# Weight work of the seven-product pairs, one step later

## The reference

```python
# block 1
ff = einsum('blf,fd->bld', square(relu(einsum('bld,df->blf', h, w_ff1))), w_ff2)   # f = 4096
# block 2
gt, up = split(h @ w1, 2, axis=-1)
y = (silu(gt) * up) @ w2                                                            # hidden width 2816
```

## Time and profile before

| | |
|---|---|
| median of 3 runs | 3332.22 us (3330.53 to 3332.47) |
| the profiled execution, its own time | 3330.85 us |
| its span | 3329.2 us |
| mean granted TensorE clock | 0.995 |
| PE busy | 3213.3 us, 97% |
| DVE busy | 1928.0 us, 58% |
| ACT busy | 1248.0 us, 37% |
| POOL busy | 910.2 us, 27% |

### The profile page before, as it was taken

The page is one execution under the profiler, slowest core; times in us unless marked ns, Lnnn a source line. Parts: engine busy times, 40 slices in busy tenths (PEclk is TensorE's granted clock), DMA queues, the critical chain, the costliest instruction groups (busy, mean ns, idle before and its releaser), DMA issues.

```text
span 3329.2 us, 40301 instructions
## 1 busy us (share of the span) xinstructions
PE 3213.3 (97%) x15473; PEld 2600.4 (78%) x15473; DVE 1928.0 (58%) x2500; ACT 1248.0 (37%) x1855; POOL 910.2 (27%) x567
## 2 busy tenths in 40 slices
PE   8999999999999999899999999999999999999997
PEld 6788777877886788777768788787788678888775
DVE  6762455444317887766653336572463587777676
ACT  3212444444325444444433333312343443334442
POOL 2111222222342222222422124341255222222214
PEclk9999999999999999999999999999999999999998
DMA  3544344325422545544424223214264223234444
GB/s 134 165 104 146 130 134 142 127 74 205 139 95 101 187 168 202 184 151 152 159 101 148 90 76 133 83 69 157 78 216 166 82 95 126 102 120 169 158 136 146
DMA packets 140906, 445.30 MB, mean 134 GB/s; under 512 B 14944, under 2 KB 24544, under 8 KB 137120
## 3 DMA queue, kind: packets, MB, share of 16 engines
q1 hardware_dynamic: 139680, 439.11, 37.9%
q10 hardware_dynamic: 1040, 3.67, 0.3%
HBM read 303.59 MB, written 142.15 MB: 134 GB/s over the span
## 4 chain that ended last, share of the span: by engine, by line
PE 50%; DVE 12%; issue 2%; ACT 2%; DMA 1%; POOL 0%; SPq 0%; DVEq 0%; ACTq 0%; POOLq 0%
PE pair L2253 24%; PE pair L332 19%; PE pair L451 3%; DVE act_lo L2455 1%; DVE f1hl L2455 1%; DVE f2hl L2455 1%; DMA w_raw<-in_stream 1%; DVE wide L2102 1%; DVE w_lo L2126 1%; PE bank L662 1%; PE wide L842 1%; PE bank L810 0%; PE wide L575 0%; PE wide L1521 0%; DVE act_lo L565 0%
## 5 line engine op out<-in xcount | busy, mean ns | idle before, releaser
L293 POOL TENSOR_TENSOR w_lo<-w_raw,w_hi 128x1024 fp32r<-128x1024 f32 (+1 forms) x184 | 392.1, 2138 | 1364.3 <-ACT w_hi L289 1323.6
L332 PE MATMUL pair<-act_hi,w_hi 128*128 128x512 f32 x1888 | 608.9, 404 | 4.3 <-DVE p L2583 1.6
L332 PE MATMUL pair<-act_lo,w_hi 128*128 128x512 f32 x1888 | 584.8, 391 | 0.0
L332 PE MATMUL pair<-act_hi,w_lo 128*128 128x512 f32 x1888 | 583.4, 390 | 0.0
L332 PEld LDWEIGHTS pair<-act_hi,w_lo 128*128 128x128 f32 x1888 | 354.6, 188 | 77.0
L332 PEld LDWEIGHTS pair<-act_lo,w_hi 128*128 128x128 f32 x1888 | 354.8, 188 | 76.7
L332 PEld LDWEIGHTS pair<-act_hi,w_hi 128*128 128x128 f32 x1888 | 334.3, 189 | 67.6 <-issue 10.3
L633 DVE TENSOR_TENSOR p<-pair,rs 128x1024 f32<-128x1024 f32 x100 | 122.3, 1223 | 390.0 <-PE pair L332 389.6
L289 ACT CAST w_hi<-w_raw 128x1024 fp32r<-128x1024 f32 x154 | 161.9, 1051 | 476.9 <-PE pair L332 423.0
L2123 POOL TENSOR_TENSOR w_lo<-w_raw,w_hi 128x512 fp32r<-128x512 f32 (+1 forms) x120 | 192.9, 1616 | 258.8 <-ACT w_hi L2116 258.8
L2253 PE MATMUL pair<-act_hi,w_hi 128*128 128x512 f32 x474 | 185.6, 392 | 2.1 <-DVE f2y L2382 1.7
(11 more groups left out here) (646 smaller groups left out, 6560.0 us busy)
## 6 DMA issues: line engine op xcount, KB each, us to landing
w_raw<-in_stream SPq DMA_DIRECT2D x275, 512.0 KB, 3.8
proj<-p SPq DMA_DIRECT2D x101, 512.0 KB, 2.6
act_lo<-hidden SPq DMA_DIRECT2D x42, 512.0 KB, 4.8
sums<-f1y SPq DMA_DIRECT2D x16, 1024.0 KB, 4.1
m2g<-proj SPq DMA_DIRECT2D x32, 512.0 KB, 5.3
sums<-f2y SPq DMA_DIRECT2D x11, 1024.0 KB, 4.1
hidden<-f1y SPq DMA_DIRECT2D x21, 512.0 KB, 3.9
hidden<-f2y SPq DMA_DIRECT2D x20, 512.0 KB, 2.6
```

The lines of the kernel that those rows point to most:

```text
L293: last = nc.gpsimd.tensor_tensor(wlo[:, slot, at:at + n], raw[:, slot, at:at + n], whi[:, slot, at:at + n].bitcast(F32), ALU.subtract)
L332: last = nc.tensor.matmul(out_pair[:, h * HALF:(h + 1) * HALF], wt, a[:, h * HALF:(h + 1) * HALF], start=k == 0 and n_pass == 0, stop=k == ...
```

## The change

```diff
         def weights_at(q, p):
 
-            if p == 6:
-                w_high(q, 0)
-                w_low(q, 0)
+            if p == 2:
+                if q > 1:
+                    w_high(q, 0)
+                    w_low(q, 0)
                 w_sum(q, 1)
-            elif p == 2:
-                if q == 1:
-                    w_sum(q, 1)
                 w_high(q, 1)
                 w_sum(q, 4)
                 w_sum(q, 2)
...
                 if q == 0:
                     for step in {3: (2,), 4: (3,), 5: (5, 4)}.get(p, ()):
                         weights_at(1, step)
+                elif q < last and opened is not None:
+                    for step in {3: (2,), 5: (3, 5), 4: (4,)}.get(p, (6,) if p == 6 else ()):
+                        weights_at(q + 1, step)
                 elif q < last:
                     weights_at(q + 1, p)
```

## The result

| | before | changed |
|---|---|---|
| median of the runs, us | 3331.42 (3325.75 to 3333.62) | 3339.76 (3338.18 to 3341.0) |
| span of the profiled execution, us | 3329.2 | 3336.5 |
| mean granted TensorE clock | 0.995 | 0.994 |

The changed kernel takes 1.0026 times as long (95% interval 1.0017 to 1.0034), 8.3 us more; the forecast was 3342, with 3337 to 3346 as its own range. Lines of the source are two lower behind the diff: the copies and readings L2264, L2266, L2381, L2382, L2454, L2455 and the matmul L2253 of before are L2262, L2264, L2379, L2380, L2452, L2453 and L2251 here.

What follows compares the result with a forecast made beforehand. TensorE, though 97% busy, was taken to wait on DVE's unbroken list up to the reading of c. 7.6 + 1.5 + 0.3 + 0.6 - 0.2 = +9.8 us: 3340.6 profiled, 3342 median; range 3337 to 3346.

Steps and rivals of the forecast that it cites:

- The mechanism: From the pair ahead to the reading of c, only the length of DVE's list decides when product 6 starts.
- The rival in which the stalls vanish: Waits ahead of product 4 and next product 0 gained, DVE's list having hidden slack: 3314 us, chance 0.07.
- the one in which only the raw-weight stall moves: All openings neutral, ACT's copy freed from the raw-weight wait: 3329.6 us, no change to speak of, chance 0.06.
- The pair ahead, +1.2: Pair before each full-size opening: sum 1 leaves DVE's idle time and meets POOL, +1.2 us, from 0 to +1.6.
- Its meeting with POOL: Pair ahead: sum 1 is held up by POOL's first-quarter subtraction and ends 0.4 us later.
- The 7 x 0.2 that the prediction works out for that rule: Added cost if POOL blocks DVE fully, one or two more blocks per opening: given as 1 us, making 3343.
- The opening pair, +0.85 - 0.15: Up to the reading of c: splits meeting POOL cost 2.05 against 1.2 us, +0.85, less 0.15 us of slack.
- the rival in which POOL loses them: First quarter and operand 3 lose their races to the splits: 0 to +4 us in all, 3332 to 3336, chance 0.22.
- The last group, +1.8: Block 2's six-tile last opening, DVE instructions shorter by a fifth: +1.5 us, and 0.3 in the pair behind it.
- The first openings, +0.3 each: First opening of either block: ACT's copy freed, raw weights 0.9 us later; net +0.3 each, bounds -2.5 to +1.5.
- The early pairs, -0.2: First three inner pairs: sum 4 starts before POOL does, shortening a chain that stalls TensorE, together -0.2 us.
- The clock, a rival at 0.15: Clock falls in the new product 6 stalls, 1.6 us each, five of seven: +8 us, 3350, chance 0.15.

Runs made afterwards that it cites:

- The four experiments that kept most of these stalls: Opening pairs shifted alone, 3337.35 us; changed kernel with pair ahead as before, 3337.44; with only sum 1 late there, 3338.53; with operand 3's quarter moved, 3343.72.
- short list with the fetch moved: Changed kernel with most weight work of full-size openings behind the reading of c, pair ahead as before, raw weights fetched right behind it: 3323.44 us, 0.9976 of before.
- fetch behind the two stores: The 3323.44 us kernel, but in block 2's first opening raw weights are fetched behind the stores of hidden row and sums: 3324.52 us, 0.9985 of before.
- short list alone: Changed kernel with most weight work of full-size openings behind the reading of c, pair ahead as before, raw-weight fetch not moved: 3330.06 us, 0.9997 of before.

## Why the prediction was right, and where it was not

**The mechanism held.** In the third opening DVE works without a break from 1504.35 to the reading of c, and its list decides when product 6 starts. The chain of waits shows it; moving the reading of c forward took the loss away (3331.29), and taking work out from ahead of it made the kernel faster than before (3323.44). The rival in which the stalls vanish fell, and so did the one in which only the raw-weight stall moves: a new stall of 2.48 us stands at product 6 (2.7 had been forecast), released by the reading at L2380, L2382 of before.

**The pair ahead, +1.2: measured +1.1 to +1.3.** Sum 1 uncovered 0.7, as the hole that grew from 1.80 to 2.63 shows. Its meeting with POOL was forecast at +0.4. Sum 1 took 1.01 instead of 0.70, and the experiment that left POOL's quarter early put the meeting at 0.3. It ends 0.56 behind POOL's end (1505.77 + 1.01 against 1504.93 + 1.29), as sum 4 did before. The Trainium skill, "SBUF — State Buffer", section "SBUF: two separate sides", calls this port an exclusive lock that blocks the loser fully; by that rule the sum would need its whole 0.70 behind POOL. The trace agrees that it is held up, not with the last 0.14 us. (The 7 x 0.2 that the prediction works out for that rule is 1.4 us, not 1.)

**The opening pair, +0.85 - 0.15: measured +0.5 to +0.7.** Both races with POOL went as forecast, so the rival in which POOL loses them fell: role 4's split takes 3.06, which is 2.35 plus 0.7 (0.95 was expected), role 6's 3.45, which is 2.35 plus the 1.1 expected, and role 5's is free. Together with the pair ahead a full-size opening costs +1.8; +1.9 was forecast. Four of them: +7.2 against 7.6.

**The last group, +1.8: measured 0.** The step that failed is the analogy "repeats the rows, shorter by a fifth". Of the three splits that count, two were met by POOL before (2.64 and 2.65, one free at 1.81), and two are now (2.39 and 2.64, one free at 1.82): 7.1 before, 6.85 after. Sum 1 cost nothing there: role 0's split in the pair ahead met less of POOL and shrank from 3.42 to 2.65, so the splits of that pair ended no later against TensorE than before.

**The first openings, +0.3 each: measured -0.8 and +0.3.** Against the matmuls around it the reading of c came 0.5 later in block 1 and 0.4 in block 2, not 0.9. The raw weights parted the two: in block 1 they came 0.2 earlier, in block 2 the forecast 0.9 later (3117.01 against 3112.54, with the matmuls ahead of the opening 3.6 later). Why they landed differently was not tested. In block 1 the rest went as written: ACT's copy (1380.63) now stands ahead of its wait for the raw weights, the stall ahead of product 4 is gone, and DVE's chain then holds product 0, beside the earlier trace rows:
```profile
1385.46 0.62 ACT L2116 CAST f1v_r<-w_raw 128x512 fp32r<-128x512 f32 x1 [4.26 <-DMA w_raw<-in_stream]
1390.08 0.47 PE L2251 MATMUL pair<-act_hi,f1v_r 128*128 128x512 f32 x1 [1.33 <-DVE f1y L2379]
```

**The early pairs, -0.2: measured -0.9.** The term had the right sign; why it is larger was not tested.

**The clock, a rival at 0.15: came in part.** The terms above add up to 5.8 us, not 9.8. Two more falls of the clock bring 3.2, and with them the total is 9.0. The prediction's number was near partly by luck: its chain was 4 us too long, most of it in the last group and the first openings, and the clock case, taken as all or nothing, paid most of it back. The price of 1.6 us for one fall was right; "five of seven" was too many in this profile: only one of the two new falls came behind a stall ahead of product 6, the other at a wait of 2.70 us ahead of a product 0. The four experiments that kept most of these stalls had two, three, two and four falls more in the networks than before (in the order of the text). The prediction also held that the clock falls where the 2.50 us occur: with the first quarter moved alone they occur in both first openings, and the clock stays at full. One execution is profiled for each kernel, but the mean granted clock of the other runs is known too, to 0.001. It averages 0.9937 over the ten runs of the changed kernel and 0.9944 to 0.9947 over those of before in the three groups. That difference times the span gives an estimate of 2.3 to 3.3 us: about two falls more are usual, and not an accident of the profiled execution. With the reading of c forward the average is 0.9947, that of its before.

## What to carry to other kernels

Where an engine works through its list without a break up to the instruction that another engine waits for, count the list, not the engine's share: an instruction that stood in an idle hole ahead of it was free, and moved behind the hole it costs its whole length, unless the move spares another instruction a meeting, as in the last group here. The cure is to put behind the deciding instruction what is not due yet, and then to look at once at what is late next; here it was a fetch, then a store behind that fetch, then the fetch again. And a stall that only moves is not neutral: the waits of 1.56 and 1.02 us never lowered the clock in these profiles, and one of 2.5 us sometimes did.

## What the runs showed of the hardware

- A stall of the same length at the same place is followed by the lower clock in one kernel and not in another: 2.48 us at clock 1.00 (15 matmuls in 3.4 us) against 2.46 us at 0.51 (8 matmuls). In the networks every fall came beside a wait of TensorE of 1.86 us or more, in all twelve profiles. Each fall lasted 3.4 us, or 6.8, and 3.4 us of it cost 1.6. What decides between them these runs do not show.
- Raw weights were in use 4.9 us after the issue when the fetch went ahead of the store of sums (1377.33 to 1382.26, short list with the fetch moved), and 7.3 us after it when it stood right behind that store (3095.87 to 3103.15, fetch behind the two stores; 1379.78 to 1387.06, short list alone).
- A sum of two quarters on DVE, 0.70 us alone, took 1.01, 1.68 and 1.80 us when a POOL subtraction ran beside it (1505.77 of the changed kernel; the earlier trace rows; 1386.21 of the changed kernel).
